# Column totals of the conditioning projection: transposes and summing copies on ScalarE in place of matmuls with a column of ones

## What is computed

```
mod = (jax.nn.silu(c) @ w_ada[i] + b_ada[i])[:, None, :]
mod_c = jax.nn.silu(c_ctx) @ w_ada[i] + b_ada[i]
sh1, sc1, g1, sh2, sc2, g2 = jnp.split(mod, N_MOD, axis=-1)
csh1, csc1, cg1, csh2, csc2, cg2 = jnp.split(mod_c, N_MOD, axis=-1)
```

## Time and profile before

| what | value |
|---|---|
| median of 3 runs | 3564.24 us (3562.53 to 3570.66) |
| profiled execution: time | 3575.23 us |
| profiled execution: span of the instructions | 3573.4 us |
| mean granted TensorE clock | 0.982 |
| PE busy | 3451.4 us, 97% |
| PE weight loads busy | 2810.8 us, 79% |
| DVE busy | 2355.6 us, 66% |
| ACT busy | 1617.9 us, 45% |
| DMA moved | 687.84 MB, 192 GB/s on average |

### The profile page before, as it was taken

How to read it: one execution, slowest core, us unless ns; L and a number is a source line. 1 busy time by engine, 2 the same in 40 slices (tenths; PEclk the granted TensorE clock), 3 DMA queues, 4 the chain that set the end, 5 groups by cost and what they waited for, 6 DMA issues and landing times.

```text
span 3573.4 us, 42859 instructions
## 1 busy us (share of the span) xinstructions
PE 3451.4 (97%) x15810; PEld 2810.8 (79%) x15810; DVE 2355.6 (66%) x2911; ACT 1617.9 (45%) x2131; POOL 33.4 (1%) x28
## 2 busy tenths in 40 slices
PE   7999999999999999999999999999887999999998
PEld 6888888887788888888878887878534788888887
DVE  5667888888766666777767663566655665656565
ACT  5555555555434545555554442444211543434343
POOL 0000000000000000000000000000000000000000
PEclk9999999999999999999999999999988999999999
DMA  7557777776676467777777753566002576667664
GB/s 237 151 175 221 225 220 226 227 229 213 224 238 205 142 188 227 226 226 230 231 220 256 252 173 96 155 195 195 1 0 96 160 221 201 220 200 222 201 220 157
DMA packets 357809, 687.84 MB, mean 192 GB/s; under 512 B 24591, under 2 KB 28704, under 8 KB 356384
## 3 DMA queue, kind: packets, MB, share of 16 engines
q1 hardware_dynamic: 357664, 685.82, 61.1%
HBM read 683.64 MB, written 2.10 MB: 192 GB/s over the span
## 4 chain that ended last, share of the span: by engine, by line
PE 69%; issue 21%; DVE 5%; ACT 2%; DMA 1%; DVEq 1%; SPq 0%; ACTq 0%; POOL 0%; POOLq 0%
PE acc L2083 16%; PE acc L2085 16%; PE acc L2084 16%; PE acc L2359 4%; PE acc L2360 4%; PE acc L2361 4%; DVE w_lo L1247 1%; DMA w_raw<-in_w_down 1%; PE turn L2290 1%; PE acc L2617 1%; PE turn L2104 1%; PE turn L2120 1%; PE acc L2583 1%; DVE ada_sum L1350 1%; PE side L2628 1%
## 5 line engine op out<-in xcount | busy, mean ns | idle before, releaser
L1247 DVE TENSOR_TENSOR w_lo<-w_raw,w_hi 128x1024 fp32r<-128x1024 f32 x708 | 838.4, 1221 | 380.4 <-ACT w_hi L771 346.2
L771 ACT ACTIVATE w_hi<-w_raw 128x1024 fp32r<-128x1024 f32 x708 | 739.0, 1062 | 718.2 <-DMA w_raw<-in_w_up 315.3
L2083 PE MATMUL acc<-w_hi,in_h 128*128 128x512 f32 x1408 | 553.0, 393 | 0.0
L2085 PE MATMUL acc<-w_hi,in_l 128*128 128x512 f32 x1408 | 548.6, 390 | 0.0
L2084 PE MATMUL acc<-w_lo,in_h 128*128 128x512 f32 x1408 | 548.0, 389 | 0.0
L2022 DVE TENSOR_TENSOR w_lo<-w_raw,w_hi 128x1024 fp32r<-128x1024 f32 x252 | 303.1, 1222 | 195.7 <-ACT w_hi L1211 187.6
L1211 ACT ACTIVATE w_hi<-w_raw 128x1024 fp32r<-128x1024 f32 x252 | 264.7, 1060 | 330.2 <-DMA w_raw<-in_w_mlp 329.8
L2359 PE MATMUL acc<-w_hi,in_h 128*128 128x512 f32 x992 | 395.9, 399 | 15.9 <-issue 6.0
L2361 PE MATMUL acc<-w_hi,in_l 128*128 128x512 f32 x992 | 390.3, 393 | 0.0
L2360 PE MATMUL acc<-w_lo,in_h 128*128 128x512 f32 x992 | 390.2, 393 | 0.0
L1350 DVE SCALAR_TENSOR_TENSOR ada_sum<-w_raw,silu_c,ada_sum 128x512 f32<-128x512 f32 x450 | 327.6, 750 | 31.7 <-issue 8.0
(11 more groups left out here) (353 smaller groups left out, 4730.1 us busy)
## 6 DMA issues: line engine op xcount, KB each, us to landing
w_raw<-in_w_up SPq DMA_DIRECT2D x352, 512.0 KB, 3.8
w_raw<-in_w_mlp SPq DMA_DIRECT2D x256, 512.0 KB, 3.7
w_raw<-in_w_in SPq DMA_DIRECT2D x200, 512.0 KB, 3.7
w_raw<-in_w_ada SPq DMA_DIRECT2D x192, 512.0 KB, 4.2
w_raw<-in_w_down SPq DMA_DIRECT2D x176, 512.0 KB, 4.8
w_raw<-in_w_o SPq DMA_DIRECT2D x64, 512.0 KB, 3.7
w_raw<-in_w_out SPq DMA_DIRECT2D x32, 512.0 KB, 3.8
x_sb<-in_x SPq DMA_DIRECT2D x1, 2048.0 KB, 7.8
```

The lines of the kernel that those rows point to most:

```text
L771: nc.scalar.activation(hi[s][:, ks], raw[s][:, ks], ACT.Copy).then_inc(w_hi[s][h], 1)
L1247: nc.vector.tensor_tensor(lo[s][:, ks], raw[s][:, ks], hi[s][:, ks].bitcast(F32), ALU.subtract).then_inc(w_lo[s][h], 1)
L2083: nc.tensor.matmul(acc[p][i][:], high(kt)[:, tok], hi[s][:, k], start=(kt == first), stop=False)
L2085: last = nc.tensor.matmul(acc[p][i][:], low(kt)[:, tok], hi[s][:, k], start=False, stop=(kt == final))
```

## The change

`ada_total` now transposes the 128 x 128 blocks of `ada_sum[0]` (and of `ada_sum[1]`) on PE into `side[0]` (and `side[1]`) and signals `ada_turned`. A new function `ada_columns` on ACT waits for that, copies each transposed block in PSUM onto itself and has the sum over its free dimension accumulated into a column of a new SBUF tile `ada_col` ([128, 8]), 8 copies for both and 4 for a single group, then drains and signals `ada_post`. `modulate` on DVE reads `ada_col` in place of `side[0]`. ACT meets `ada_columns` in "up" after `centre(before, 1)` and ahead of `split_up(3)`, and in "dn" after the `split_hi` of the same (c, i), which is that of the product two later; at (0, 0) that is ahead of `centre(NPAIR - 1, 1)`.

```diff
+    ada_col = st("ada_col", 8)
...
-    ada_post, ada_mod = sem("ada_post"), sem("ada_mod")
+    ada_post, ada_mod, ada_turned = sem("ada_post"), sem("ada_mod"), sem("ada_turned")
...
+        def ada_columns(i, both):
+
+            act_.wait_ge(ada_turned, i + 1)
+            n = 2 if both else 1
+            for f in range(4):
+                for c in range(n):
+                    block_ = side[c][:, f * P:(f + 1) * P]
+                    nc.scalar.activation(block_, block_, ACT.Copy, accum_out=ada_col[:, n * f + c:n * f + c + 1])
+            act_.drain().then_inc(ada_post, 1)
...
                     centre(before, 1)
+                if total is not None:
+                    ada_columns(total, l == 0)
                 split_up(3)
...
                 split_hi(*later_place(l, "dn", 0, i, 2))
+                if (0, i) in DN_TOTAL:
+                    ada_columns(l * ADA_LAYER + DN_TOTAL[0, i], l * ADA_LAYER + DN_TOTAL[0, i] < ADA_BOTH)
...
                     split_hi(*later_place(l, "dn", c, i, 2))
+                    if (c, i) in DN_TOTAL:
+                        ada_columns(l * ADA_LAYER + DN_TOTAL[c, i], l * ADA_LAYER + DN_TOTAL[c, i] < ADA_BOTH)
...
-                nc.vector.tensor_tensor(mod[:, ds(i * 4, 4)], side[0][:, 0:8].rearrange("p (f c) -> p f c", c=2),
+                nc.vector.tensor_tensor(mod[:, ds(i * 4, 4)], ada_col[:].rearrange("p (f c) -> p f c", c=2),
...
-                nc.vector.tensor_tensor(mod[:, ds(i * 4, 4), 0], side[0][:, 0:4], b_ada[:, ds(i * 4, 4)], ALU.add).then_inc(ada_mod, 1)
+                nc.vector.tensor_tensor(mod[:, ds(i * 4, 4), 0], ada_col[:, 0:4], b_ada[:, ds(i * 4, 4)], ALU.add).then_inc(ada_mod, 1)
...
-            for f in range(4):
-                for c in range(n):
-                    last = nc.tensor.matmul(side[0][:, n * f + c:n * f + c + 1], ada_sum[c][:, f * P:(f + 1) * P], one[:], start=True, stop=True)
-            last.then_inc(ada_post, 1)
+            for c in range(n):
+                for f in range(4):
+                    last = nc.tensor.transpose(side[c][:, f * P:(f + 1) * P], ada_sum[c][:, f * P:(f + 1) * P], ident[:])
+            last.then_inc(ada_turned, 1)
```

## The result

The changed kernel takes 3627.62 us (median of 4 runs, 3623.22 to 3631.69), the kernel before 3563.39 us beside it (4 runs, 3562.07 to 3570.66): a ratio of 1.0176, 95% interval 1.0155 to 1.0196. It is 64 us slower, where 7.8 us less was forecast.

The account below looks back on a forecast made before the run. PE was taken to bound the kernel, busy 97% of the span; its 10.4 us saving, less waits place by place, summed to 7.8 us: 3564.24 - 7.8 = 3556.4 us. Forecast's own range 3553 to 3560, overall range 3550 to 3567.

Parts of the forecast that it names:

- Rival (a): On ACT at the both totals: summing copies at 0.82 us a block become the wait; 3574.6 us; chance 0.10.
- the low end: ACT's summing copies: 0.28 us a block, the lower of two ends, the other being 0.82.
- rival (b): Slack at (1, 5) of layer 0, or copies ready sooner: all 10.4 us stay, 3553.8 us; chance 0.15.
- Transposes: On PE at every total: eight transposes in 0.99 us replace 16 passes in 1.79; 10.4 us saved in all.
- Rival (d): PE's new transposes run at the faster spacing, 0.65 us for eight: gain 12.3, 3551.9 us; chance 0.03.
- "up" of layer 0: Five both totals in "up": copies hold up nothing, the lead of 1.9 us falls to 1.1; gain 4.0 us.
- rival (c): In "up" of layer 0 DVE, not PE, sets the pace: 3.2 us remain, 3561.0 us; chance 0.20.
- "up" of layer 1: Five single totals in "up", with more room everywhere: 0.4 us each, gain 2.0 us.
- (0, 0) of layer 0: Both total in "dn": copies delay conv activations and DVE 3.9 us, PE waits 0.2; gain 0.6 us.
- (1, 5) of layer 0: Both total in "dn": late copies hold DVE 1.2 us in a chain without slack, PE's 0.8 lost; result -1.2 us.
- the single (3, 8): Single total in "dn" of layer 0: 0 to 0.1 us of holding; gain 0.4 us.

Follow-up runs that it names:

- e2: The kernel before with only an unused 32-byte tile in the place where ada_col stands; 3638.91 us, ratio 1.0205.
- e1: The change whole, but with ada_col behind the last SBUF tile so that nothing is shifted; 3557.84 us, ratio 0.9977 to the kernel before.
- m1: The same edit as e1, run once more beside m2; 3556.44 us, ratio 0.997 to the kernel before.
- h1: e1 with ACT's summing copies moved: behind the conv activations at (0, 0), ahead of split_hi at two later "dn" places; 3556.56 us, ratio 0.9974.
- m2: The same edit as h1, run once more beside m1; 3555.74 us, ratio 0.9963 to the kernel before.
- k3: The kernel before with one stationary tile alone, mix_l[1], moved up by 32 bytes; 3563.7 us in one run.

## Why the prediction was wrong, and where it was right

**The step that failed: a line at no cost.** The prediction goes through the work that the change removes, adds and moves, and says of `modulate`'s new source, the only place where `ada_col` comes into it, "`modulate` reads SBUF instead of PSUM at the same size: nothing". The cost of the tile's place is not in the sum: 32 bytes more between the ring and the stationary operands were put at nothing without a word, and no row of before could have priced them. Measured alone (e2) they are 1.0205 times, 74 us. With the forecast's own gain of 7.8 beside it that makes +66, and +64 was measured; after and e1, measured at different times, differ by 3627.62 - 3557.84 = 69.8 us. That is less than the 79 us of 13152 periods. A part of the difference is waiting that the slower PE no longer has to do: in the products' weight loads idle stretches of over 0.15 us sum up to 48 us in before and to 39 in e2.

**Slower, but not by the rival that said so.** Rival (a), the price of a summing copy, had 0.10. The copies cost the low end: period 0.28 us (0.27 the activation, 0.19 the read of the sum, overlapping on both sides). That is well below the 0.51 from which (a) decided. The Trainium skill, "ScalarE: Activation LUTs", section "Step-by-step: what each stage is for", calls PSUM the lower-latency destination; the copies in PSUM, 268 ns, are slightly shorter than the copy of 277 ns to SBUF, which agrees but does not prove it.

**The sum, without the shift.** e1 is the change that the prediction thought it had before it. By the medians it is -6.7 us (3557.84 against 3564.53), in m1 -9.4 (3556.44 against 3565.82), for a forecast of -7.8. The intervals are wide, -11.4 to -4.6 and -14.6 to -6.8: they bear the forecast out, but they do not tell it from the 10.4 of rival (b). The places in the trace do.

- *Transposes.* Taken at 0.99 us for eight, they took 0.88: the saving is 0.91 and not 0.80 for a both total. Rival (d), the spacing of 81 ns in the Trainium skill, "TensorE: Matmul & The Clock Gate", section "Back-to-back issue gap", would be 0.65; the trace shows 0.110 each, closer to the row of 0.124 than to the page.
- *"up" of layer 0.* Forecast -4.0. In e1 PE stands 5.0 us ahead of before at 820 us, of which 0.15 were there before the first total: 4.9 gained. No new wait: rival (c) is out. *"up" of layer 1.* Each single total shows -0.45, 2.2 in all for 2.0 forecast.
- *(0, 0) of layer 0.* Forecast 0.2 us of waiting for the remainder of product 3. PE meets it, in e1, with the weight load

```profile
835.39 0.19 PEld L2101 LDWEIGHTS acc<-w_hi,ah 128*128 128x128 f32 x1 [0.29 <-issue]
```

  where before it went through the earlier trace rows. That is 0.3, near the 0.2 of the forecast. (The view puts it to "issue"; DVE's remainder of that half, which starts at 834.06 and takes 1.2, ends 0.1 before.) But DVE stays late, and PE waits at three more halves (0.15 and 0.9 us in chunk 0, and 1.2 us more at 909.96, where before waited 0.3 already), which the prediction did not look for, since it ended at product 3. From 5.0 ahead, PE comes to the total of (1, 5) 3.6 ahead: this place cost 1.4 where a gain of 0.6 was forecast. It is the term of the sum that was most off. In h1, with the copies behind the conv activations, the waits in chunk 0 are not there.
- *(1, 5) of layer 0.* Forecast: DVE held 1.2 us and the stall of 941.80 longer by that and by PE's head start. Held: 1.06 us, above. The stall in e1:

```profile
939.64 0.77 PE L2101 MATMUL acc<-w_hi,ah 128*128 128x512 f32 x1 [2.36 <-DVE w_lo L1265]
```

  2.36 us instead of the 1.63 of before:

```profile
941.80 0.50 PE L2083 MATMUL acc<-w_hi,ah 128*128 128x512 f32 x1 [1.63 <-DVE w_lo L1247]
```

  PE's head start over before goes from 3.6 us ahead of the total (4.5 behind it) to 941.80 - 939.64 = 2.2, most of it at three halves before this one. So the stall itself is only 0.7 longer, and the place cost 1.4 for 1.2 forecast. The chain of DVE, slot, DMA and ACT was read rightly: rival (b) is out.
- *Rest.* At the last weight load before layer 1's first total PE is at

```profile
1401.24 0.19 PEld L2101 LDWEIGHTS acc<-w_hi,in_h 128*128 128x128 f32 x1
```

  for 1404.42 before: 3.2 us ahead, 3.0 of them gained in layer 0, where 4.6 were forecast (4.0 + 0.6 - 1.2 + 0.8 + 0.4 for the single (3, 8)). Layer 1 brought 4.3 for 3.2, but about 1.1 of it is the clock, at half for 6.8 us at 1865 us in before and for 3.4 in e1. So the places gave some 6.2 us for 7.8, and that the medians of e1 and m1 lie on both sides of 7.8 is in part luck.

So the mechanism that was argued was right in most steps and its size close, but for (0, 0). What set the result was not among the cases, and the chance for a slower kernel was given to the only mechanism that had been thought of.

## What to carry to other kernels

Where PE sets the pace, an edit that allocates anything is also an edit of addresses: keep the distance of the stationary to the moving operands (here a whole multiple of 256 bytes), put a new small tile behind the last one, and run the pad alone, in the kernel before, to price it. When a small change moves the whole program, compare the spacing of an untouched inner loop first: two rows showed 0.227 and 0.232 us here. And compare two executions stage by stage, with the granted clock beside it: of the 6.5 us between m1 and m2 only 3.1 were the change's, and a later stretch at half clock hid them.

## What was not expected of the hardware

- The fast-format matmuls of 128 x 512, each with its weight load, repeat every 0.227 us when the stationary operands stand a multiple of 256 bytes from the ring, and every 0.232 to 0.233 us at the other distances tried. The whole kernel is then 1.6 to 2.1% longer. The weight loads themselves are no longer (0.19 us in both), only their spacing is.
- One operand of three off that distance slows a group as much as all three (k3: 0.019 us).
- In a row of summing copies the second instruction of each, 0.19 us, costs next to nothing (period 0.283 us, the activation alone 0.268).
- Thirty-two matmuls that no kernel here touched took 19.1 or 25.3 us (m1 and m2), by how long the granted clock stayed down in them. Among the seven profiled executions at before's speed those with the long form took 3572.65 to 3575.23 us, the others 3559.75 to 3565.82.
